# Gated delta rule on one core: eight heads unrolled, the next head's k projected one head ahead, two heads' triangular levels in shared TensorE groups

## What is computed

```python
proj = h @ w_in                       # q, k, v, gate per head, and two small columns
qkv = silu(causal_dwconv(qkv, conv_w))          # 4 taps
q = l2norm(q) * 128 ** -0.5;  k = l2norm(k)
G = cumsum(g);  decay = exp(where(causal, G_i - G_j, -inf))
tri = where(strict, beta * (k k^T) * decay, 0) + I
sol = triangular_solve(tri, [v * beta, k * beta * exp(G)])      # u, w
qk = (q k^T) * decay
def step(S, ...):                     # over the chunks
    v_new = u - w @ S
    o = (q * exp(G)) @ S + qk @ v_new
    S = chunk_decay * S + (k * exp(G_last - G))^T @ v_new
o = rmsnorm(o, g) * silu(gate)
h = h + o @ w_out
```

## Time and profile before

| what | us |
|---|---|
| three runs: median, lowest, highest | 1358.7, 1358.55, 1360.52 |
| the profiled execution's own time | 1359.78 |
| its span, first to last instruction | 1358.0 |
| TensorE busy | 1329.8 (98%) |
| VectorE busy | 774.3 (57%) |
| ScalarE busy | 595.0 (44%) |
| mean granted TensorE clock | 0.995 of 2.4 GHz |

### The profile page before, as it was taken

How to read it: one execution, slowest core, us unless ns; L and a number is a source line. 1 busy time by engine, 2 the same in 40 slices (tenths; PEclk the granted TensorE clock), 3 DMA queues, 4 the chain that set the end, 5 groups by cost and what they waited for, 6 DMA issues and landing times.

```text
span 1358.0 us, 21831 instructions
## 1 busy us (share of the span) xinstructions
PE 1329.8 (98%) x8313; PEld 1064.6 (78%) x8313; DVE 774.3 (57%) x1152; ACT 595.0 (44%) x930; POOL 0.2 (0%) x4
## 2 busy tenths in 40 slices
PE   7899999999999999999999999999999999999998
PEld 5677777777788888888887777778888888888886
DVE  6687888887464343343456666676543443434555
ACT  5555566555454132242346566654431432313442
POOL 0000000000000000000000000000000000000000
PEclk9899999999999999999999999999999999999999
DMA  4321322221333333333234322224333233333323
GB/s 156 95 62 50 76 62 77 62 77 48 106 97 108 93 93 109 88 97 99 87 97 129 116 63 62 62 78 155 94 98 103 85 102 93 108 93 93 93 81 105
DMA packets 42341, 124.02 MB, mean 91 GB/s; under 512 B 3952, under 2 KB 12720, under 8 KB 41776
## 3 DMA queue, kind: packets, MB, share of 16 engines
q1 hardware_dynamic: 33472, 116.95, 28.7%
q10 hardware_dynamic: 8816, 6.33, 2.3%
HBM read 119.04 MB, written 4.23 MB: 91 GB/s over the span
## 4 chain that ended last, share of the span: by engine, by line
PE 93%; DVE 3%; ACT 2%; issue 1%; DMA 1%; ACTq 0%; SPq 0%; DVEq 0%
PE acc L331 27%; PE acc L333 26%; PE acc L332 26%; PE ps L483 1%; PE ps L453 1%; PE ps L676 1%; PE ps L703 1%; PE ps L691 1%; PE ps L426 1%; DMA work<-rows 1%; ACT wh L300 1%; DVE wl L307 1%; PE ps L331 1%; PE ps L714 1%; PE ps L333 0%
## 5 line engine op out<-in xcount | busy, mean ns | idle before, releaser
L331 PE MATMUL acc<-xh,wh 128*128 128x512 f32 x1008 | 418.3, 415 | 12.4 <-DVE xl L1870 8.6
L333 PE MATMUL acc<-xh,wl 128*128 128x512 f32 x1008 | 396.0, 393 | 0.0
L332 PE MATMUL acc<-xl,wh 128*128 128x512 f32 x1008 | 395.3, 392 | 0.0
L300 ACT ACTIVATE wh<-raw 128x1024 fp32r<-128x1024 f32 x207 | 216.8, 1050 | 186.3 <-DMA raw<-in_weights 168.2
L307 DVE TENSOR_TENSOR wl<-raw,wh 128x1024 fp32r<-128x1024 f32 x207 | 252.9, 1222 | 65.5 <-ACT wh L300 62.5
L331 PE MATMUL acc<-yh,wh 128*128 128x512 f32 x608 | 238.1, 392 | 0.0
L332 PE MATMUL acc<-yl,wh 128*128 128x512 f32 x608 | 236.6, 389 | 0.0
L333 PE MATMUL acc<-yh,wl 128*128 128x512 f32 x608 | 236.6, 389 | 0.0
L331 PEld LDWEIGHTS acc<-xh,wh 128*128 128x128 f32 x1008 | 190.6, 189 | 55.3 <-DVE wl L307 11.0
L333 PEld LDWEIGHTS acc<-xh,wl 128*128 128x128 f32 x1008 | 190.5, 189 | 41.0
L332 PEld LDWEIGHTS acc<-xl,wh 128*128 128x128 f32 x1008 | 191.0, 189 | 37.8 <-issue 4.3
(11 more groups left out here) (247 smaller groups left out, 1099.1 us busy)
## 6 DMA issues: line engine op xcount, KB each, us to landing
raw<-in_weights SPq DMA_DIRECT2D x208, 512.0 KB, 3.5
work<-rows ACTq DMA_DIRECT2D x16, 256.0 KB, 7.1
h<-in_xT SPq DMA_DIRECT2D x4, 512.0 KB, 6.4
proj<-work ACTq DMA_DIRECT2D x2, 1024.0 KB, 4.2
work<-proj SPq DMA_DIRECT2D x2, 1024.0 KB, 6.8
outT<-h SPq DMA_DIRECT2D x8, 256.0 KB, 2.4
cst<-in_cst SPq DMA_DIRECT2D x1, 512.0 KB, 3.3
work<-in_pT SPq DMA_DIRECT2D x1, 512.0 KB, 4.8
```

What stands on the lines that cost most here:

```text
L300: nc.scalar.activation(slot(u)[0][:], raw[u.const % 2][:], ACT.Copy).then_inc(hi_done, 1)
L331: nc.tensor.matmul(dst[:], hi, mh[:, k, :], start=(n == 0), stop=False)
L332: nc.tensor.matmul(dst[:], hi, ml[:, k, :], start=False, stop=False)
L333: mm = nc.tensor.matmul(dst[:], lo, mh[:, k, :], start=False, stop=(n == KT - 1))
```

## The change

- Head 0's k **and** head 1's k are projected first. The unit order becomes k0, then per pass i: k of head i+1, q, v, gate of head i (with the numbering from `u_k`, `u_q`, `u_v`, `u_g`). The total of k-steps is the same.
- The six levels of a head are cut in two halves of three. In pass i the group r (0, 1, 2) does level 4, 5, 6 of head i-1 (*late*) and level 1, 2, 3 of head i (*early*), in one run of matmuls on TensorE. Before pass 1 stand three early groups of head 0 alone (`pe_first_steps`).
- The early levels work on packed 32x32 diagonal blocks: 128x64 masks and 128x128 transposes on VectorE, in place of 128x256 and 128x512. Level 6 uses tiles of 64 rows by 32 columns.
- The norm sum becomes two matmuls of rounded halves, `osh` (ScalarE, L1043) and `osl` (VectorE, L1794), against rounded ones. It follows the second tx group.
- k by token is copied to SBUF (`ktoks`, L1008) so that its PSUM bank is free; decay, exp(G), k and the row norms have two buffers each.
- Tables of the head (`tcur`, `cwc`, `tcg`) go, since the head number is a constant: all passes are written out, with no hardware loop.
- The semaphore increment `level_go` ahead of every small group goes.

The core of the diff:

```diff
-            return ([x(1), tx(1), vtr] + [s for n in range(2, 7) for s in (x(n), tx(n))]
-                    + [w] + [s for c in range(C) for s in (v(c), os(c))] + ([] if project else [norm]))
+            return ([x(0), tx(0), vtr, x(1), tx(1), x(2), tx(2), w] + [s for c in range(C) for s in (v(c), os(c))]
+                    + ([] if early else [norm]))
...
-        FILL = [0, 2, 2, 0, 2, 2, 2, 2, 2, 2, 2, 2, 2, 1, 1, 1, 1, 1, 1, 1, 1, 1, 1]
-        FIRST_FILL = [6, 2, 2, 0, 1, 2, 1, 2, 1, 2, 1, 2, 1, 1, 1, 1, 1, 1, 1, 1, 1, 1, 0]
+        FILL = [2, 2, 0, 2, 2, 2, 2, 3, 2, 2, 2, 2, 2, 2, 2, 3]
+        FIRST_FILL = [2, 1, 1, 1, 1, 1, 1] + [2, 2, 0, 1, 2, 1, 2, 1, 2, 1, 2, 1, 2, 1, 2, 2]
+        SHORT_FILL = [2, 2, 0, 1, 2, 1, 2, 2, 1, 2, 1, 2, 1, 2, 1, 2]
+        LAST_FILL = [1, 2, 0, 1, 2, 1, 2, 1, 1, 1, 2, 1, 2, 1, 2, 5, 10]
...
+        def pe_norm(pe, j):
+            pe.wait_ge(osh_d, j + 1)
+            nc.tensor.matmul(ps[4][:], ones_r, osh, start=True, stop=False)
+            pe.wait_ge(osl_d, j + 1)
+            nc.tensor.matmul(ps[4][:], ones_r, osl, start=False, stop=True).then_inc(oss_d, 1)
...
+            if early:
+                Lt, Ti = Lts[e % 2], Tis[e % 2]
+                pe.wait_ge(te_d, 4 * e + r + 1)
+                for c in range(C):
+                    for lo in range(0, P, 32):
+                        q = slice(lo, lo + 32)
+                        last = nc.tensor.matmul(blk32(ps[2], c)[q], ch(Lt, c)[q, q], blk32(Ti, c)[q],
+                                                start=True, stop=True)
...
             def w():
-                pe.wait_ge(tt_d, i * 6)
+                pe.wait_ge(ttl_d, 3 * i)
...
-                if project:
-                    pe_ktr(pe, i)
+                if i + 1 < H:
+                    pe_ktr(pe, i + 1)
```

More of the change, by code:

```diff
@@ L439, in vtr, with x, tx @@
                 last.then_inc(vtr_d, 1)
-            def small_tile():
-                pe.sem_inc(level_go, 1)
-            def x(n):
+            def x(r):
+                return lambda: x_group(pe, i, r, True, early)
+            def tx(r):
                 def step():
[L447 to L464, removed]
@@ new lines, in units @@
+            def units():
+                for n in range(5):
+                    yield from unit_steps(pe, Unit(n), xh, xl, x_gate if n == 0 else None)
+            todo = units()
+            gates = dict(zip((8, 12, 17, 21), pe_gate_steps(pe)))
+            for n in range(5 * KT):
+                if n in gates:
+                    gates[n]()
+                if n == KT:
+                    pe.wait_ge(s_keep, 16)
+                    pe.wait_ge(x_sq, KT - 1)
+                    nc.tensor.matmul(ps[0][:], ones, accb, start=True, stop=True).then_inc(rs_mm, 1)
+                if n == KK_FIRST_AT:
+                    pe_ktr(pe, 0)
+                    pe_kk(pe, 0)
+                next(todo)
@@ new lines, in pe_start, with pe_period, pe_gdn, units @@
+            for _ in todo:
+                pass
+            pe_qk(pe, 0)
+        KK_FIRST_AT = 32
+        def pe_period(pe, i, fill, steps, todo):
+            for step, n in zip(steps, fill):
+                step()
+                for _ in range(n):
+                    next(todo)
+        def pe_gdn(pe):
+            def units(i):
+                for n in range(4 * i + 1, min(4 * i + 5, 4 * H)):
+                    yield from unit_steps(pe, Unit(n), xh, xl)
+            pe_start(pe)
+            todo = units(1)
+            for _ in range(FIRST_FILL[0]):
+                next(todo)
+            pe_period(pe, 1, FIRST_FILL[1:], pe_first_steps(pe) + pe_head_steps(pe, 1), todo)
+            for _ in todo:
+                pass
+            for i in range(2, H):
+                todo = units(i)
+                pe_period(pe, i, FILL if i < H - 1 else SHORT_FILL, pe_head_steps(pe, i), todo)
@@ new lines, in dve_gdn @@
+            dve_updates(dve, i, 1, True, early)
+            split_lo(dve, Unit(first + 1))
+            if early:
+                dve_masks(dve, i, 2, True, early)
+            if i + 1 < H:
+                dve_take_head(dve, 1, i + 1)
+            dve_updates(dve, i, 2, True, early)
+            if b > 0:
+                dve_o1(dve, b)
+            if i + 1 < H:
+                for _ in dve_taps(dve, 1, i + 1):
+                    pass
+            if b > 0:
+                dve_yb(dve, b)
@@ L1577, in dve_gdn, with dve_osl @@
             state(1)
[L1578 to L1580 removed]
+            if early:
+                next(q_taps)
+                next(q_taps)
+                split_lo(dve, Unit(first + 3))
             state(2)
[L1582 to L1584 removed]
+            if early:
+                dve_take_head(dve, 2, i)
+                for _ in dve_taps(dve, 2, i):
+                    pass
+        def dve_osl(dve, i):
+            dve.wait_ge(osh_d, i)
+            if i > 1:
+                dve.wait_ge(oss_d, i - 1)
+            nc.vector.tensor_tensor(osl, osq, osh.bitcast(F32), ALU.subtract).then_inc(osl_d, 1)
```

1042 lines of the change are left out of this document (578 added, 464 removed).

## The result

The changed kernel takes **1427.2 us** (median of 4 runs, 1423.7 to 1428.45) against 1358.65 beside it: ratio 1.0503, 95% interval 1.0486 to 1.052. It is slower, as forecast, and by twice as much: the forecast was 1393, its range ended at 1413. The profiled execution's span is 1426.6 us in place of 1358.0.

The account below looks back on a forecast made before the run. TensorE was taken to bound the middle passes. Savings from merged groups and norm, outweighed by +37 us of waiting for Silu, smaller waits and slow clock, summed to +34.5 on 1359.8: 1393 us, range 1371 to 1413.

Parts of the forecast that it names:

- "issue" inside the small groups: Sign of being wrong: TensorE waiting for instructions inside small groups, a wait at another place than the k transposes.
- The wait for Silu: TensorE idle before the next k's transposes behind w: 7.4 us in passes 2 to 6, +37; pass 1 +1.5.
- The rivals without this wait: Shared groups decide and Silu of k is in time, so passes keep only smaller waits: 1345 us, 8%.
- without its slow clock: The wait comes without a slow clock behind it, or merged groups' second halves are nearly free: 1375 us, 12%.
- The merged groups: TensorE's small groups in the levels: early and late halves share one entry, -13.4 us, bounds -24 to 0.
- Code: TensorE's instruction loads: loop entry's break goes (-2.0), two more breaks of 1.54 come, one in the old's place: net +1.1 us.
- the bound of +15: Upper bound of the term for TensorE's instruction loads, whose net was +1.1 us and lower bound -3.6.
- The rival on code loads: Every written-out pass is new code; loads break one small group in three, some 12 breaks of 1.54: 1408 us, 12%.
- The clock: Slow TensorE clock behind each wait for Silu: 1.9 us, five times, +9.5; 0 to 17 in all.
- The copy for level 6: ScalarE's copy stands behind the tap of k, so TensorE waits 0.6 us in each of six passes: +3.6.
- The norm's two parts: Two rounded matmuls for the norm sum save 0.4 us eight times, -3.2; the second's wait costs 0.5 six times, +3.0.
- The start: First passes, 30 to 140 us: idle and slow clock of 14.5 us before become 11.3, waits 2.4 and 5.5 included: -3.2.

Follow-up runs that it names:

- The run with Silu first: Changed kernel with ScalarE's Silu of the next k right behind the level 6 copy, and VectorE's k taps ahead of the last update: 1394.1 us, ratio 1.0241.
- the filled wait: Changed kernel with rows in 2 KB pieces, plus 28 unneeded matmuls before the k transposes in passes 2 to 6: 1395.8 us, against 1409.4 without them.
- the third order: Changed kernel with Silu of next k earlier, 2 KB rows, side-engine work reordered, next k transposed behind the three units after w: 1362.2 us, ratio 1.0031.
- the pair of runs: Changed kernel, Silu of next k earlier, 2 KB rows, second reordering of side engines: 1371.5 us with the split norm sum, 1368.3 with one fp32 matmul.
- the first and third orders: The first: changed kernel, Silu of next k earlier, 2 KB rows, five further moves on ScalarE and VectorE: 1367.0 us, ratio 1.0061; the third: 1362.2 us.

## Why the prediction was right and wrong

The direction and its first cause were right, and the time was 34 us too low. The prediction named "issue" inside the small groups as a sign of being wrong, and four of the five breaks are there. By its own terms:

- **The wait for Silu:** +38.5 forecast (five of 7.4 and 1.5), 36.8 measured, at the line named, with the chain named. The run with Silu first takes it away. The rivals without this wait (1345 us) or without its slow clock (1375) are refuted by the waits and by the filled wait. Pass 1 has 0.7 of the 1.5, and pass 2, which follows a break, 6.0 of the 7.4.
- **The merged groups:** 0.84 and 1.07 us forecast. The group with level 4, from 309.44 to 311.70 with two k-steps between, is 0.865; that with level 6, from 324.01 to 327.35 less the wait of 0.73, 1.21. Seven passes of 4 x 0.03 + 2 x 0.14 are 2.8 us: -10.6 in place of -13.4, which fits the 12 us of the third order. The group that is dearest is the one that changes from tiles of 64x32 to 32x32 inside, which is the direction of the Trainium skill's sentence on drains (TensorEngine Tiling (Array Packing), Key Properties); its 0.35 over the others was 0.23 before, with no change inside. That leaves 0.12 for the change of tiles, if 16 matmuls on 64x32 tiles cost what 8 on 64x64 did, which no run shows.
- **Code, the step that failed first.** "I take two more breaks of 1.54": there were five, of 2.6 to 4.8 us, 17.0 in all and +13.4 net against +1.1. I had priced a break by the two I saw and counted them by guess. What was missed is the cause: a load of code waits behind the transfer of the rows, which the prediction knew at 7.94 us. A break is as long as what is left of that transfer when TensorE runs out of code (0.4 to 2.5 us), and 2.2 to 2.3 more. The +13.4 lie within the bound of +15, but that bound left out the clock behind the breaks. The rival on code loads had the right direction, but many short breaks where there were few long ones. The sentence of the Trainium skill (Runtime: NRT & Kernel Launch, Instruction fetch mechanics) that straight code mostly hides its fetch holds for the kernel before when unrolled (1.0003, with one new break of 1.6 us), and not for the changed one, until the rows are in larger pieces.
- **The clock, the second.** +9.5 was for the waits, 1.9 each; the filled wait shows 2.7 each, 13.6. The breaks, which the term did not have at all, bring slow stretches of their own: up to 15.5 us, by half of TensorE's busy time in them. All told 32 us are lost at 1.2 GHz, 27 more than before, where the prediction's bound for the waits was 17.
- **The copy for level 6:** +3.6 forecast for passes 2 to 7; L550 waits 3.3 there, and 1.4 in pass 1. Before, such waits were 1.9 in all.
- **The norm's two parts:** -3.2 + 3.0 forecast. The listed waits are 3.2, and the second matmul's short ones are mostly below what that list shows. The saving of 0.4 a head is there only where the second matmul needn't wait. In the pair of runs the split costs some 3 us instead of saving 0.2.
- **The start:** the waits I placed there were 2.4 and 5.5; they are 2.5 (v of head 0, released by L1527) and 2.3 (the transpose, L1598). The second ends at 67.69 us, near the 67 forecast; TensorE stood before it at 65.44 and not at 61.5, in part since the break of 2.6 us had held it up on the way. The clock there was worse than two slow stretches. The term was also reckoned wrong: the 9.5 us of idle time before contain the breaks of 1.54 and 2.02, which the term for code counts once more. Counted once, the sum would have been some 1397 us.

The spans differ by 68.6 us, 59.0 idle and 9.6 busy. By the lists of waits, each less what it was before, the idle part is 36.6 for Silu, 13.4 for the breaks, 3.2 for the norm, 2.8 for the copy of level 6 and 3 for small ones. The busy part is 27 for the clock and -10.6 for the merged groups; that makes 16, so 7 us are not placed. Halving may count the clock too high here: in the first and third orders, with little slow clock, the same reckoning leaves 11 to 12 us of work saved.

What stays open: why the unrolled kernel before rides over the same loads (the counts above fit, no run isolates them), and whether some order of ScalarE and VectorE brings out the 11 us or so that the merged groups take from TensorE. Three did not. One part was not tried: merged groups with k at its old distance.

## What to carry to other kernels

An order on a side engine costs nothing until a consumer moves in front of it: when work is merged or moved a stage ahead, walk the chain of every operand of the first instruction behind it, and put what it needs first on each engine. Look for small-piece transfers beside dense small instructions, since loads of code can wait behind them; here larger pieces were worth 0.2% to the kernel before and 18 us to the changed one. And price a wait of TensorE with its clock: 7.5 us of idleness cost 10.2.

## What the hardware showed that I had not expected

- In each break of the changed kernel a load of 16 KB of code started within 0.25 us of the end of a broadcast of 1056 packets, and TensorE went on 2.2 to 2.3 us later; with the same bytes in pieces of 2 KB the breaks fell from 17.0 to 0.2 us in all.
- 140 matmuls more made a kernel 13.6 us faster, since the granted clock stayed near 2.4 GHz: 0.99 in place of 0.91 over the passes.
- Writing out six passes of the loop of the kernel before cost nothing: 1358.5 us, with 56 packets of code for 37.
